# The state-space branch of a three-block decoder: channels on the partitions, its chunks placed between the gate's projections

## What is computed

```
xbc = silu(causal_conv4(xbc) + conv_b);  xs, B, C = split(xbc)      # 512 | 2*128 | 2*128 channels
dt  = softplus(dt + dt_bias);            a_cs = cumsum(dt * -exp(a_log)) within a chunk
xdt = xs * dt
y_diag[l] = sum_{s<=l} (C_l . B_s) * exp(a_cs[l] - a_cs[s]) * xdt[s]
state_c   = sum_s B_s * exp(a_cs[last] - a_cs[s]) * xdt[s]
prev      = prev * exp(a_cs[last]) + state_c        # from chunk to chunk
y_off[l]  = (C_l . prev) * exp(a_cs[l])
y   = y_diag + y_off + xs * d_skip
out = rmsnorm(y * silu(z), g_norm)                  # over the 512 channels
```

## Time and profile before

| what | us |
|---|---|
| median of 3 runs (lowest to highest) | 3607.71 (3601.76 to 3613.13) |
| the profiled execution, its own time | 3595.51 |
| its span, first to last instruction | 3593.7 |
| PE busy in the span | 3265.5 (91%) |
| PEld busy | 2599.9 (72%) |
| DVE busy | 2034.7 (57%) |
| ACT busy | 1299.3 (36%) |
| POOL busy | 375.4 (10%) |

### The profile page before, as it was taken

The page is one execution under the profiler, slowest core; times in us unless marked ns, Lnnn a source line. Parts: engine busy times, 40 slices in busy tenths (PEclk is TensorE's granted clock), DMA queues, the critical chain, the costliest instruction groups (busy, mean ns, idle before and its releaser), DMA issues.

```text
span 3593.7 us, 51778 instructions
## 1 busy us (share of the span) xinstructions
PE 3265.5 (91%) x21422; PEld 2599.9 (72%) x21422; DVE 2034.7 (57%) x3609; ACT 1299.3 (36%) x2143; POOL 375.4 (10%) x334
## 2 busy tenths in 40 slices
PE   6898899999898999998996888879999889989998
PEld 4667778887685688886765666567777677768886
DVE  5445467754433476755545437688778763554444
ACT  3234242222323342223432135465555533333321
POOL 0001100000000000000001000055445420000000
PEclk9898899999998999999997989999999989999999
DMA  3220034432230134432220120211111103223231
GB/s 128 62 71 1 16 103 141 141 129 88 75 101 24 53 112 146 141 112 77 94 71 18 48 94 25 68 53 41 45 39 38 51 5 106 82 95 104 94 96 68
DMA packets 297352, 274.77 MB, mean 76 GB/s; under 512 B 10400, under 2 KB 287008, under 8 KB 296352
## 3 DMA queue, kind: packets, MB, share of 16 engines
q1 hardware_dynamic: 292864, 256.07, 22.3%
q10 hardware_dynamic: 4256, 15.40, 1.2%
HBM read 265.16 MB, written 6.29 MB: 76 GB/s over the span
## 4 chain that ended last, share of the span: by engine, by line
PE 80%; DVE 10%; ACT 5%; issue 3%; POOL 1%; DMA 0%; DVEq 0%; ACTq 0%; SPq 0%; POOLq 0%
PE ps L95 79%; DVE f L107 3%; DVE f L101 2%; DVE r L101 2%; PE ps L98 2%; ACT f L88 1%; ACT f L92 1%; ACT r L92 1%; POOL f L101 1%; DVE f L104 1%; ACT f L89 1%; DVE f L113 1%; ACT L88 1%; DVE f L110 1%; DVE r L107 0%
## 5 line engine op out<-in xcount | busy, mean ns | idle before, releaser
L95 PE MATMUL ps<-r,r 128*128 128x512 f32 x10368 | 2443.8, 395 | 110.6 <-DVE r L101 71.4
L95 PEld LDWEIGHTS ps<-r,r 128*128 128x128 f32 x10368 | 1933.4, 191 | 565.3 <-issue 140.2
L95 PE MATMUL ps<-f,f 64*64 64x64 f32 (+9 forms) x10116 | 769.5, 267 | 173.7 <-ACT f L92 45.8
L101 DVE TENSOR_TENSOR r<-f,r 128x1024 fp32r<-128x1024 f32 (+2 forms) x621 | 656.1, 1063 | 433.4 <-ACT r L92 427.9
L95 PEld LDWEIGHTS ps<-f,f 64*64 64x64 f32 (+3 forms) x10116 | 586.9, 157 | 344.1 <-issue 162.4
L92 ACT ACTIVATE r<-f 128x1024 fp32r<-128x1024 f32 (+2 forms) x548 | 506.7, 937 | 764.3 <-PE ps L95 649.7
L101 POOL TENSOR_TENSOR f<-f,f 128x256 f32<-128x256 f32 (+1 forms) x276 | 332.3, 1217 | 472.6 <-ACT f L88 263.7
L107 DVE SCALAR_TENSOR_TENSOR f<-f,f,f 128x128 f32<-128x128 f32 (+3 forms) x622 | 365.5, 593 | 26.4 <-ACT f L88 7.3
L101 DVE TENSOR_TENSOR f<-ps,f 128x512 f32<-128x512 f32 (+7 forms) x333 | 180.3, 554 | 336.0 <-PE ps L95 326.6
L92 ACT ACTIVATE f<-ps 128x256 f32<-128x256 f32 (+3 forms) x422 | 183.4, 451 | 514.3 <-PE ps L95 366.4
L88 ACT ACTIVATE f<-ps 128x512 f32<-128x512 f32 (+3 forms) x203 | 111.9, 553 | 586.6 <-PE ps L95 584.6
(11 more groups left out here) (33 smaller groups left out, 733.8 us busy)
## 6 DMA issues: line engine op xcount, KB each, us to landing
f<-in_w_mlp_up SPq DMA_DIRECT2D x32, 1024.0 KB, 6.0
f<-in_w_mlp_down SPq DMA_DIRECT2D x32, 1024.0 KB, 6.3
...
```

The source lines that it names most:

```text
L95: return self.e.matmul(out, l, r, start=first, stop=last)
L101: return self.e.tensor_tensor(out, a, b, op)
```

## The change

- The gate z is projected with channels on the partitions, as four tiles (`Weights.tile`) in place of `lin_tm`.
- The x tiles come in another order: B and C first, then xs. Softplus and the product with -exp(a_log) are done between x tiles 1 and 5.
- The exponents are no longer differences of cumulative sums: POOL makes LD = strict triangle * (dt*a) (128x1024) per chunk, and a matmul with U sums what lies between the two tokens; Exp is taken straight from PSUM, and the triangle is applied to C.B (128x256) and not to M. The same trick gives both decays to the chunk's end in one bank (dec), and for chunks 1 to 3 exp(a_cs) for all channels (EB, eight matmuls with 64 stationary columns).
- The order on PE is written out: decay 0 and 1 behind x tiles 6 and 7; after z tile 0 the transposes of chunks 0 and 1; after z 1 the outputs of chunk 0, decay 2, transposes 2; after z 2 outputs 1, decay 3, transposes 3; after z 3 outputs 2 and 3.
- y1 and y2 come out with channels on the partitions, so the transposes back are gone; the state starts without a zeroed buffer, and two buffers take turns.
- The fence inside the stage is gone; at the closing fence PE only signals and goes on (`pass_fence`).
- Skip term and product with z are eight DVE operations of 128x512 in NSA's stream, behind the low half for the second c tile. The squares are taken by ACT (four, behind Sin), added by POOL (three), summed over channels by one matmul with ones in front of the gl tile; Sqrt on ACT, reciprocal 128x512 and four products on DVE follow between gl and the ga tiles.

The diff, cut to its core (allocations, semaphore counts, the split of the softplus helpers into halves, and the bodies that go, are left out):

```diff
-        pe.fence()
+        pe.pass_fence()
         self.nsa.pe(pe)
...
+    TILES = (4, 5, 6, 7, 0, 1, 2, 3)
-        for n in range(8):
-            G.tile(pe, ("ssd.x", n), W, 2328 + n * 128, 128, X, [("ssd_pad", n + 1)])
-            if n == 0:
+        for i, n in enumerate(self.TILES):
+            G.tile(pe, ("ssd.x", i), W, 2328 + n * 128, 128, X, [("ssd_pad", i + 1)])
+            if i == 0:
...
-        G.lin_tm(pe, "ssd.z", W, 1816, 512, X, lambda tt, b: [("ssd_z", tt + 1)])
-        f = lambda ap: ap.rearrange("p a b -> p (a b)")
-        pe.wait_ge("ssd_dta", 1)
-        b = self.bank["acs"] = K.ps.take(pe, ("ssd_acs", 1))
...
-        pe.fence()
-        for c, p in waves(4, 4):
...
+            elif i == 5:
...
+                b = self.bank["dec"] = K.ps.take(pe, ("ssd_dec", 1))
+                pe.mm(K.ps.t[b][:, 0:32], self.strict, f, True, True)
+                K.mm_done(pe.mm(K.ps.t[b][:, 32:64], K.ones, f, True, True), "ssd.dec")
+            elif i > 5:
+                self.decay_pe(pe, i - 6)
+        after = ((self.turn_pe, 0), (self.turn_pe, 1)), ((self.out_pe, 0), (self.decay_pe, 2), (self.turn_pe, 2)), (
+            (self.out_pe, 1), (self.decay_pe, 3), (self.turn_pe, 3)), ((self.out_pe, 2), (self.out_pe, 3))
+        for n in range(4):
+            G.tile(pe, ("ssd.z", n), W, 1816 + n * 128, 128, X, [("ssd_z", n + 1)])
+            for step, c in after[n]:
+                step(pe, c)
+    def decay_pe(self, pe, c):
+        cs = slice(c * 128, c * 128 + 128)
+        pe.wait_ge("ssd_LD", c + 1)
+        for g in range(2):
+            b = self.bank["M", c, g] = K.ps.take(pe, ("ssd_M", 2 * c + g + 1))
+            for e in range(4):
+                t = pe.mm(K.ps.t[b][:, e * 128:e * 128 + 128], LD[:, 4 * g + e, :], K.U, True, True)
+            K.mm_done(t, ("ssd.M", c, g))
+        if c:
+            b = self.bank["EB", c] = K.ps.take(pe, ("ssd_EB", c))
+            for h in range(8):
+                t = pe.mm(K.ps.t[b][h % 2 * 64:h % 2 * 64 + 64, h // 2 * 128:h // 2 * 128 + 128],
+                          self.dta[:, c, h:h + 1].broadcast_to((128, 64)), K.U, True, True)
+            K.mm_done(t, ("ssd.EB", c))
+        pe.wait_ge("ssd_xbc", 4)
+        b = self.bank["CB", c] = K.ps.take(pe, ("ssd_CBU", c + 1))
+        for g in range(2):
+            t = pe.mm(K.ps.t[b][:, g * 128:g * 128 + 128], self.xbc[:, 4 + g, cs], self.xbc[:, 6 + g, cs], True, True)
+        K.mm_done(t, ("ssd.CB", c))
+    def turn_pe(self, pe, c):
+        b = self.bank["xs", c] = K.ps.take(pe, ("ssd_xdt", c + 1))
+        for i in range(4):
+            t = pe.tr(K.ps.t[b][:, i * 128:i * 128 + 128], self.xbc[:, i, cs], K.ident)
+        K.mm_done(t, ("ssd.xs", c))
+        if c < 3:
+            b = self.bank["B", c] = K.ps.take(pe, ("ssd_B", c + 1))
+            for g in range(2):
+                t = pe.tr(K.ps.t[b][:, g * 128:g * 128 + 128], self.xbc[:, 4 + g, cs], K.ident)
+            K.mm_done(t, ("ssd.B", c))
+    def out_pe(self, pe, c):
+        if c < 3:
+            pe.wait_ge("ssd_B", c + 1)
+            pe.wait_ge("ssd_xdd", c + 1)
+            b = self.bank["st", c] = K.ps.take(pe, ("ssd_prev", c + 1))
+            for g in range(2):
+                t = pe.mm(K.ps.t[b][:, g * 256:g * 256 + 256], Bt[:, g * 128:g * 128 + 128], xdd[:, g * 256:g * 256 + 256], True, True)
+            K.mm_done(t, ("ssd.st", c))
+        pe.wait_ge("ssd_MM", c + 1)
+        pe.wait_ge("ssd_xdt", c + 1)
+        b = self.bank["y1", c] = K.ps.take(pe, ("ssd_y", c + 1))
+        for h in range(8):
+            hp = slice(h % 2 * 64, h % 2 * 64 + 64)
+            t = pe.mm(K.ps.t[b][hp, h // 2 * 128:h // 2 * 128 + 128], xdt[:, h * 64:h * 64 + 64], M[:, h, :], True, True)
+        K.mm_done(t, ("ssd.y1", c))
+        if c:
+            pe.wait_ge("ssd_prev", c)
+            b = self.bank["y2", c] = K.ps.take(pe, ("ssd_a", c))
+            for i in range(4):
+                t = pe.mm(K.ps.t[b][:, i * 128:i * 128 + 128], self.prev[c % 2][:, i * 128:i * 128 + 128], self.xbc[:, 6 + i // 2, cs],
+                          True, True)
...
+            if i == 1:
+                act.wait_ge("ssd_ysum", 1)
+                softplus_exp_act(K, act, self.y, self.e)
+                act.f(self.na, K.pv("a_log_2"), ACT.Exp).then_inc(S("ssd_na"), 1)
+            elif i == 2:
+                softplus_ln_act(K, act, self.w, self.l)
+            elif i > 5:
+                self.decay_act(act, i - 6)
+        for n in range(4):
+            k = ("ssd.z", n)
             G.act(act, k)
...
-        act.fence()
...
+            act.f(self.z[:, n, :], G.at[k], ACT.Silu).then_inc(S("ssd_z"), 1)
+            if n == 0:
+                self.turn_act(act, 0)
+                self.turn_act(act, 1)
+            elif n == 1:
+                self.decay_act(act, 2)
+                self.turn_act(act, 2)
+            elif n == 2:
+                self.decay_act(act, 3)
+    def decay_act(self, act, c):
+            act.f(self.dec.rearrange("p a b -> p (a b)"), K.ps.t[self.bank["dec"]][:, 0:64], ACT.Exp).then_inc(S("ssd_dec"), 1)
+        if c >= 2:
+            act.wait_ge("mm", K.done["ssd.y1", c - 2])
+        for g in range(2):
+            act.wait_ge("mm", K.done["ssd.M", c, g])
+            act.f(M[:, 4 * g:4 * g + 4, :], blocks(K.ps.t[self.bank["M", c, g]][:, :], 4), ACT.Exp).then_inc(S("ssd_M"), 1)
+        if c:
+            if c == 3:
+                act.wait_ge("ssd_a", 1)
+            act.wait_ge("mm", K.done["ssd.EB", c])
+            act.f(EB, K.ps.t[self.bank["EB", c]][:, :], ACT.Exp).then_inc(S("ssd_EB"), 1)
+    def turn_act(self, act, c):
+        act.wait_ge("mm", K.done["ssd.B", c])
+        if c == 2:
+            act.wait_ge("mm", K.done["ssd.st", 0])
+        act.cp(self.sets[c % 2][5], K.ps.t[self.bank["B", c]][:, 0:256]).then_inc(K.S("ssd_B"), 1)
...
+        dve.ts(self.strict, K.U, -1.0, 1.0, MUL, ADD).then_inc(S("ssd_strict"), 1)
...
-            dve.wait_ge("ssd_pad", n + 1)
-            b, q = self.pads[n % 3], self.xbc[:, n, :]
+            elif i == 2:
+                softplus_w_dve(K, dve, 2, f(self.dt), self.e, self.w)
+            elif i == 4:
+                dve.own(softplus_end_dve(K, dve, 2, self.y, f(self.dt), self.e, self.w, self.l))
+                dve.settle()
+                dve.wait_ge("ssd_na", 1)
+                dve.stt(f(self.dta), f(self.dt), -1.0, self.na, MUL, MUL).then_inc(S("ssd_dta"), 1)
+            elif i == 7:
+                self.decay_dve(dve, 0)
+            dve.wait_ge("ssd_pad", i + 1)
...
-        dve.fence()
+        for n in range(4):
+            G.dve(dve, ("ssd.z", n))
+            if n == 0:
+                self.decay_dve(dve, 1)
+                self.turn_dve(dve, 0)
+                self.turn_dve(dve, 1)
+            elif n < 3:
+                self.out_dve(dve, n - 1)
+                self.decay_dve(dve, n + 1)
+                self.turn_dve(dve, n + 1)
+            else:
+                self.out_dve(dve, 2)
+                self.out_dve(dve, 3)
+    def decay_dve(self, dve, c):
+        M = self.sets[c % 2][1].rearrange("p (g e) t -> p g e t", g=2)
+        dve.wait_ge("mm", K.done["ssd.CB", c])
+        dve.wait_ge("ssd_MM", c)
+        dve.tt(self.CBU, blocks(K.ps.t[self.bank["CB", c]][:, 0:256], 2), K.U.unsqueeze(1).broadcast_to((128, 2, 128)), MUL).then_inc(
+            S("ssd_CBU"), 1)
+        dve.wait_ge("ssd_M", 2 * c + 2)
+        dve.wait_ge("ssd_CBU", c + 1)
+        dve.tt(M, M, self.CBU.unsqueeze(2).broadcast_to((128, 2, 4, 128)), MUL).then_inc(S("ssd_MM"), 1)
+    def turn_dve(self, dve, c):
+        LD, M, EB, xdt, xdd, Bt = self.sets[c % 2]
         h3 = lambda ap: blocks(ap, 8)
         up = lambda c: each(c, 8, 64)
+        if c >= 2:
+            dve.wait_ge("mm", K.done["ssd.y1", c - 2])
+        dve.wait_ge("mm", K.done["ssd.xs", c])
+        dve.tt(h3(xdt), h3(K.ps.t[self.bank["xs", c]][:, :]), up(self.dt[:, c, :]), MUL).then_inc(S("ssd_xdt"), 1)
+        if c < 3:
+            dve.wait_ge("ssd_xdt", c + 1)
+            dve.wait_ge("ssd_dec", 1)
+            dve.tt(h3(xdd), h3(xdt), up(self.dec[:, 0, 8 * c:8 * c + 8]), MUL).then_inc(S("ssd_xdd"), 1)
+    def out_dve(self, dve, c):
+        EB, o = self.sets[c % 2][2], self.o[:, 4:8, c * 128:c * 128 + 128]
+        P = lambda *k: K.ps.t[self.bank[k]][:, :]
+        new, old = self.prev[(c + 1) % 2], self.prev[c % 2]
+        if 0 < c < 3:
+            dve.wait_ge("ssd_prev", c)
+            if c == 2:
+                dve.wait_ge("mm", K.done["ssd.y2", 1])
+            dve.own(dve.tt(blocks(new, 8), blocks(old, 8), each(self.dec[:, 1, 8 * c:8 * c + 8], 8, 64), MUL))
+            dve.settle()
+        if c < 3:
+            dve.wait_ge("mm", K.done["ssd.st", c])
+            if c == 0:
+                dve.cp(new, P("st", c)).then_inc(S("ssd_prev"), 1)
             else:
+                dve.tt(new, new, P("st", c), ADD).then_inc(S("ssd_prev"), 1)
+        dve.wait_ge("mm", K.done["ssd.y1", c])
```

(46 more changed lines are left out.)

229 lines of the change are left out of this document (55 added, 174 removed).

## The result

| | before | after |
|---|---|---|
| median of 5 runs (lowest to highest) | 3610.16 (3601.76 to 3613.13) | 3571.39 (3568.25 to 3589.05) |
| ratio, 95% interval | | 0.9905 (0.9877 to 0.9933) |
| profiled execution, its span | 3595.51, 3593.7 | 3568.84, 3567.0 |
| granted clock over the span | 0.948 | 0.950 |

Faster by 38.8 us between the medians and by 34.3 (24 to 44) by the ratio; the forecast was 3566.7, in a range of 3552 to 3586. The two profiled executions lie only 26.7 apart. The difference has to be read from the stages, and by them one term of the sum was too small and one cost had not been foreseen.

What follows compares the result with a forecast made beforehand. Latency bounded the chunks (75.7 us between the last z matmul and NSA's first), a cast chain the projections. Terms -47.3 + 2.7 + 0.9 + 2.0 + 0.7 = -41.0 us, from 3607.7 to 3566.7; range 3552 to 3586.

Steps and rivals of the forecast that it cites:

- The main term: Stage up to NSA's first matmul: chunk work becomes 24.9 us of PE work among the tiles, saving 47.3 us.
- The form with 64 columns: EB and y1 matmuls, 64-column stationary: 0.95 us per group of 16 pieces, 6.7 for seven; otherwise 6.7 more.
- rival 4: Chunk steps among z tiles: products come late, PE waits some 8 us a chunk; near -10 us, 3598; chance 0.03.
- rival 5: From x tile 3 on: gaps keep PE at 1.2 GHz, +80 on -43, 3645 us, slower than before; chance 0.02.
- POOL beside DVE: Convolutions 4 to 7: POOL's LD products slow DVE on the cast chain; +0.7 us, between 0 and 2.8.
- The cast chain's other gaps: PE gaps from work behind Silu: 2.2 us at x tile 3, 2.4 at 4, 0.8 at 6, 1.4 at z 1.
- the net: PE's idle gaps from x 0 to z 3: 8.8 us after against 5.2 before, so +3.6.
- Clock, +2.0: Gaps ahead of x tiles 3 and 4 may let PE's clock fall: +2.0 us, between 0 and 5.0.
- The fence side, +2.7: NSA's first matmul to q 1: 30.0 us in place of 27.3, with eight moved operations filling DVE's idle time.
- The variance matmul: In front of gl: two pieces of 512 columns on PE, +0.9 us.
- rival 3: Cast chain: each of four ACT table loads costs another 1.4 us, 5.6 in all; 3572 us; chance 0.04.
- rival 1: Projections: idle gaps double again (+9) and the clock falls twice more (+5); -27 us, 3581; chance 0.15.

Runs made afterwards that it cites:

- c2: c1 with q 1's cast and low half ahead of NSA's position tables, and the norm's squares ahead of Sin; median 3548.48 us, ratio 0.9849 against the kernel before.
- e2: The changed kernel with the four LD products on DVE in place of POOL; median 3562.29 us, ratio 0.9901 against the kernel before.
- c1: The changed kernel with LD products on DVE, NSA's v projections ahead of k's turning products, small ACT/DVE work moved into waits; median 3548.73 us, ratio 0.9853 against before.
- e1: The changed kernel run once more with no edit; median 3574.04 us, ratio 0.9915 against the kernel before.
- b1: The changed kernel with skip term and product with z put back in front of the stage's end; median 3566.04 us, ratio 0.9887 against the kernel before.
- b6: The kernel before with the triangle applied to C.B on DVE in place of POOL's product on the decay matrix; median 3596.56 us, ratio 0.9977 against before.

## Why the prediction was right, and where not

**The main term** held: the chunk work as packed PE work. With the clock and POOL, 44.6 us were forecast to NSA's first matmul, and 39.75 came. Busy PE time in the chunks fell from 46.5 (75.6 us at a clock of 0.70) to 25.65, against 24.9 reckoned. The form with 64 columns was priced right: M and EB together take 2.97, M alone 1.95, so 1.02 a group for 0.95. No wait over 0.6 us stands inside the chunk steps, so rival 4 did not occur, and neither did rival 5.

**"POOL beside DVE: 0.7, upper end 2.8" was the term that failed.** The forecast priced a hit at 0.7 us, from one row, and took one hit in the sum and four as the upper end. A hit is longer where POOL's instruction is longer: DVE lost 3.03 us beside 4.44 of POOL, 1.52 beside 1.90, and 1.17 where the two overlapped for 1.32 (1876.28 to 1877.60), in all 5.7 us, 1.4 a product. PE's gaps grew by 3.0 at x tile 6 and 0.9 at z tile 1, so PE lost 3.9 of the 5.7. The Trainium skill ("SBUF — State Buffer", SBUF: two separate sides) says that the port pair is locked for the whole instruction, also against a DVE operation with two SBUF inputs. The operations stretched here have two SBUF inputs, and the 16 additions with a PSUM input take 6.15 beside POOL and 6.13 alone: the trace agrees on which are hit. In size the loss stayed under a full block: the first three operations lay beside POOL for 4.0 us (1849.68 to 1853.70) and lost 3.03. Two SBUF inputs are not needed for it: in c2 four operations with one SBUF input took 2.66 for 1.69 beside POOL.

**The cast chain's other gaps**: 2.10, 2.06 and 0.81 (in e2) against 2.2, 2.4 and 0.8 reckoned. At z tile 1 1.4 were reckoned, and 2.8 stay without POOL: the cast waits behind ACT's table load and exponentials (1882.18 to 1885.05, below), and in c1, which moves them, the gap is gone. In the whole, idle time among the tiles rose by 8.9 us (3.57 to 12.47) where the net was put at 3.6. Both ends of that count were off: it gave 8.8 for the changed kernel, and 5.2 for the kernel before, where the earlier trace rows had 3.6 to read. With 0.75 of PE work and 1.6 of clock that makes S to N 113.5 (77.35 to the last z matmul before, + 25.65 + 8.9 + 1.6); the trace has 113.34.

**Clock, +2.0**: in the stage 1.6 in the first trace (x tile 6) and 4.2 in e1 (with z tile 1), inside its bounds. With the v projection the clock cost 12.8 us in the first trace, far outside them.

**The fence side, +2.7**: 28.79 for 27.29, so +1.5. The cover named for the eight operations is there, and b1 prices its loss at 0.67. The variance matmul took 1.07, 0.9 reckoned. **Table switches**: rival 3 is false. ACT after:

```profile
1882.18 1.28 ACT L88 ACT_TABLE_LOAD   x1
1883.48 1.57 ACT L88 ACTIVATE f<-ps 128x512 f32<-128x512 f32 x3
```

Exp starts 1.30 us behind the start of the load. Of rival 1 a part came, and it came from POOL more than from the table loads and the clock.

**What no case had**: the 11.2 us of the v projection, a stretch at the lower clock behind a wait that the kernel before has too. Against the forecast's own reference the profiled execution is 14.3 us late: +4.8 in the stage, -1.2 to q 1, +11.3 behind, -0.6 elsewhere. That the median still came within 4.7 us is in part luck: before's profiled execution lay 12 to 15 us under its median and after's only 2.6, and this made up for most of it.

**Where the gain comes from**: 39.75 us to NSA's first matmul. 20.8 are PE's busy time in the chunks (fewer pieces, full clock) and the rest idle time. Taken alone the norm is 11.3, the mask 2.5, the z tiles as cover 2.3, the fence none. They don't add up to the whole. That the old loop had two chains side by side, and a shorter one of the two hardly shows while the other is there, is a reading of b6 and was not tested with both shortened. How the remaining part divides between the transposes back, the cumulative sums, the softplus wait of 5.73 and the clock was not taken apart.
